# Attention scores of the first block in split-precision passes, differential maps combined before the transposes, and q/k made head by head

## The reference, cut to what matters

```python
s = jnp.einsum("bhcqd,bhcsd->bhcqs", qb, k_b).astype(jnp.float32) * scale_b
p = jax.nn.softmax(s, axis=-1)
a = p[:, :, 0] - lam * p[:, :, 1]
return jnp.einsum("bhqs,bhsv->bhqv", a.astype(v_b.dtype), v_b)
```

## Time and profile before

| what | value |
|---|---|
| median of three runs | 3435.35 us |
| span of the profiled execution | 3426.4 us |
| difference of the two, taken as what lies around the span | 8.95 us |
| TensorE busy | 3252.0 us, 95% of the span |
| VectorE busy | 1119.9 us, 33% |
| ScalarE busy | 995.3 us, 29% |
| GpSimd busy | 279.3 us, 8% |
| share of TensorE in the chain that ended last | 89% |

### The profile page before, as it was taken

One profiled execution on the slowest core, in us unless ns is written; L12 is line 12 of the kernel. 1 busy time (PEld: TensorE's weight loads), 2 busy tenths in 40 slices (PEclk: granted clock), 3 DMA queues, 4 the chain that ended last, 5 costly groups with the idle time before them and its releaser, 6 DMA issues.

```text
span 3426.4 us, 35084 instructions
## 1 busy us (share of the span) xinstructions
PE 3252.0 (95%) x14020; PEld 2219.0 (65%) x14020; DVE 1119.9 (33%) x1827; ACT 995.3 (29%) x1607; POOL 279.3 (8%) x268
## 2 busy tenths in 40 slices
PE   7999998999989999989999999979998999989997
PEld 6866564888878656658887555544666433468886
DVE  2624332333226343233332233344333100043322
ACT  4355441222233545322221223333222100022222
POOL 4480000000032700000000000000000000000000
PEclk8999999999989999999999999989998999989999
DMA  4221121333222211123323201102111121123331
GB/s 105 79 80 38 38 75 37 99 98 88 85 82 76 74 38 53 47 78 96 93 84 92 80 14 36 37 1 62 37 37 50 25 74 49 49 62 98 95 90 62
DMA packets 340274, 221.98 MB, mean 65 GB/s; under 512 B 8364, under 2 KB 334892, under 8 KB 340112
## 3 DMA queue, kind: packets, MB, share of 16 engines
q1 hardware_dynamic: 337360, 214.65, 21.6%
q0 software_dynamic: 2224, 2.99, 0.8%
q10 hardware_dynamic: 528, 2.10, 0.2%
HBM read 217.62 MB, written 2.10 MB: 64 GB/s over the span
## 4 chain that ended last, share of the span: by engine, by line
PE 89%; DVE 5%; ACT 4%; issue 1%; DMA 1%; DVEq 0%; ACTq 0%; SPq 0%
PE ps L591 83%; PE ps L602 4%; PE ps L618 2%; DVE R L1691 1%; ACT R L1204 1%; DVE xL L1687 0%; DVE x_lows L1687 0%; DMA ident<-in_c_ident 0%; PE ps L945 0%; DMA R<-in_ctx 0%; ACT R L1200 0%; ACT L1193 0%; DVE R L1780 0%; DVE R L1762 0%; DVE wL L1713 0%
## 5 line engine op out<-in xcount | busy, mean ns | idle before, releaser
L591 PE MATMUL ps<-R 128*128 128x64 f32 (+6 forms) x2272 | 519.6, 372 | 29.5 <-ACT R L1204 8.7
L591 PEld LDWEIGHTS ps<-R 128*128 128x128 f32 (+3 forms) x2272 | 306.1, 192 | 243.8 <-issue 137.1
L591 PE MATMUL ps<-xH,wH 128*128 128x512 f32 x1056 | 417.5, 395 | 21.9 <-DVE xL L1687 21.9
L591 PE MATMUL ps<-U,ring 128*128 128x512 f32 (+5 forms) x960 | 406.8, 575 | 12.3 <-ACT R L1410 12.3
L1204 ACT ACTIVATE R<-ps 128x512 f32<-128x512 f32 (+9 forms) x504 | 248.7, 493 | 578.7 <-PE ps L591 514.6
L591 PE MATMUL ps<-xL,wH 128*128 128x512 f32 x1056 | 414.2, 392 | 0.0
L591 PE MATMUL ps<-xH,wL 128*128 128x512 f32 x1056 | 414.0, 392 | 0.0
L591 PE MATMUL ps<-R,ring 128*128 128x512 f32 x704 | 367.2, 676 | 2.9 <-DVE R L1927 1.6
L1354 ACT ACTIVATE wH<-raws 128x2048 fp32r<-128x2048 f32 (+1 forms) x114 | 192.9, 1692 | 569.0 <-PE ps L591 568.4
L591 PEld LDWEIGHTS ps<-U,ring 128*128 128x128 f32 (+2 forms) x960 | 179.6, 191 | 214.7 <-issue 189.5
L1713 DVE TENSOR_TENSOR wL<-raws,wH 128x2048 fp32r<-128x2048 f32 (+1 forms) x114 | 229.3, 2011 | 233.2 <-ACT wH L1354 226.3
(11 more groups left out here) (279 smaller groups left out, 3281.8 us busy)
## 6 DMA issues: line engine op xcount, KB each, us to landing
raws<-in_w_gate_up SPq DMA_DIRECT2D x88, 512.0 KB, 5.1
ring<-in_w_in SPq DMA_DIRECT2D x36, 1024.0 KB, 6.2
ring<-in_w_ada SPq DMA_DIRECT2D x24, 1024.0 KB, 5.1
raws<-in_w_down SPq DMA_DIRECT2D x32, 704.0 KB, 4.6
raws<-in_w_ffn_in SPq DMA_DIRECT2D x44, 512.0 KB, 5.2
ring<-in_w_in SPq DMA_DIRECT2D x34, 512.0 KB, 5.7
raws<-in_w_ffn_out SPq DMA_DIRECT2D x16, 704.0 KB, 4.7
ring<-in_w_o SPq DMA_DIRECT2D x5, 1280.0 KB, 5.9
```

The costliest lines, as they stand in the source:

```text
L591: return nc.tensor.matmul(o, a, b, start=first, stop=last)
```

## The change: what it does

1. **Scores.** q and k are kept in `QK_parts` as a high and a low part of type float32r. For diff and gqa (width 64) q's high part stands on rows 0 to 63 and its low part on rows 64 to 127 (for the other map of a diff head, the other way round); k's high part is copied to both halves of one slot and its low part to both halves of the next. A score tile is then two passes over 128 rows. For mla (width 96) it is three passes over 96 rows. The one float32 matmul of before goes.
2. **Diff maps.** The stage has 16 steps of two units. VectorE multiplies the second map's exponentials by a ratio and adds the first's (`combined`); then there is one set of transposes, one of copies and one of value products for both maps. `PX` has 4 buffers where `P3` had 3.
3. **q and k streamed.** The three bursts go. A head's q or k (an "item") is transposed into a bank of the D ring; ScalarE copies the high parts out (2 copies for a diff q, 4 for a diff k, 1 for a gqa q, 2 for a gqa k, 1 for mla) and VectorE then subtracts as many low parts. `items_beside` says at which step: diff heads 1 to 3 at steps 0, 1, 4, 5, 8 and 9 of the diff stage; gqa between the tiles of the `mla_w_uq` products; mla at steps 22 and 23 of gqa, at the start of mla and at 8 of its steps.
4. **Order.** gqa's pieces of `W_IN` come before the latents; the diff stage comes before the `mla_w_uq` and `mla_w_ukv` products; four modulation pieces are loaded before these two. A score waits only for its own bank (`score_bank`). The squares and the norm of the diff output are spread over steps of gqa and mla.

The diff, cut to its core:

```diff
+        def high_copies(item):
+            kind, h = item
+            if kind == "diff_q":
+                o = B_SLOTS[h % 2]
+                return [(r, r, o + c) for c, r in enumerate(HALVES)]
+            if kind == "diff_k":
+                o = B_SLOTS[h % 2] + 2
+                return [(r, to, o + 2 * c) for c, r in enumerate(HALVES) for to in HALVES]
+            if kind == "gqa_q":
+                return [(HALVES[0], HALVES[0], G_SLOTS[0] + h)]
+            if kind == "gqa_k":
+                return [(HALVES[0], to, G_SLOTS[1] + 2 * (h - GH)) for to in HALVES]
+            return [((0, AQK), (0, AQK), A_SLOTS[h % 2][0 if kind == "mla_q" else 2])]
+        def low_parts(item):
+            kind, h = item
+            out_ = []
+            for n, (r, to, slot_) in enumerate(high_copies(item)):
+                if kind in ("diff_q", "gqa_q"):
+                    out_.append((r, r, slot_, HALVES[1] if r == HALVES[0] else HALVES[0], slot_))
+                elif kind in ("diff_k", "gqa_k"):
+                    out_.append((r, r, slot_, to, slot_ + 1))
+                else:
+                    out_.append((r, r, slot_, r, slot_ + 1))
+            return out_
+        def items_beside(stage, j):
+            if stage == "diff":
+                h, t = j // TT + 1, j % TT
+                return b_items(h)[t:t + 1] if h < BH and t < 2 else []
+            if stage == "gqa":
+                return a_items(0)[j - 22:j - 21] if j >= 22 else []
+            h, t = (j + 7) // TT, (j + 7) % TT
+            return a_items(h)[t:t + 1] if 2 <= h < AH and t < 2 else []
...
-        W_IN = (quarter_pieces("diff_qk", c1, 2 * BH * BV) + quarter_pieces("latent", 0, c1)
-                + quarter_pieces("diff_v", c1 + 2 * BH * BV, BH * BV)
+        W_IN = (quarter_pieces("diff_qk", c1, 2 * BH * BV)
                 + quarter_pieces("gqa_q", c1 + 3 * BH * BV, GH * GD)
-                + quarter_pieces("gqa_kv", c1 + 3 * BH * BV + GH * GD, 2 * GK * GD))
+                + quarter_pieces("gqa_kv", c1 + 3 * BH * BV + GH * GD, 2 * GK * GD)
+                + quarter_pieces("latent", 0, c1)
+                + quarter_pieces("diff_v", c1 + 2 * BH * BV, BH * BV))
...
+            for a in range(4):
+                yield ada_piece(l * NADA + a)
...
+            def part_transposes(item):
+                kind, h = item
+                bank = db.fill(pe)
...
+                    ins = nc.tensor.transpose(bank[0:v_.shape[1], t * P:(t + 1) * P], v_, ident[:, :])
+                ins.then_inc(d_full, 1)
+                qk_banks.append(db.n)
+            def stacked_scores(o, q, t, k):
+                mm(o, QKP[:, q, t * P:(t + 1) * P], QKP[:, k, :], True, False)
+                return mm(o, QKP[:, q, t * P:(t + 1) * P], QKP[:, k + 1, :], False, True)
+            def split_scores(o, slots, t):
+                qh, ql, kh, kl = slots
+                mm(o, QKP[0:AQK, qh, t * P:(t + 1) * P], QKP[0:AQK, kh, :], True, False)
+                mm(o, QKP[0:AQK, ql, t * P:(t + 1) * P], QKP[0:AQK, kh, :], False, False)
+                return mm(o, QKP[0:AQK, qh, t * P:(t + 1) * P], QKP[0:AQK, kl, :], False, True)
...
+            def score_bank(u):
+                if u >= 3:
+                    pe.wait_ge(s_exp, u - 2)
+                return S_BANKS[u % 3][:, :]
...
+            def attend_diff():
+                nonlocal unit
+                u0, made = unit, len(qk_banks)
+                rows_taken = modulation()
+                def scores(i):
+                    h, c, t = i // 8, i % 2, i // 2 % 4
+                    pe.wait_ge(qk_ready, made + 2 * h + 2)
+                    o = B_SLOTS[h % 2]
+                    stacked_scores(score_bank(u0 + i), o + c, t, o + 2 + 2 * c).then_inc(s_full, 1)
+                for item in b_items(0):
+                    part_transposes(item)
+                for i in range(3):
+                    scores(i)
...
+                for j in range(N):
+                    if 2 * j + 3 < 2 * N:
+                        scores(2 * j + 3)
+                    pp.more(combined)
+                    transposes([PX[(u0 + 2 * j) % 4][:, s * P:(s + 1) * P] for s in range(TT)], P)
+                    transposed.append(ab.n)
+                    if 2 * j + 4 < 2 * N:
+                        scores(2 * j + 4)
+                    if j >= 1:
+                        values(j - 1, None, (VB + (j - 1) // TT * BV, VB + ((j - 1) // TT + 1) * BV), transposed)
+                    for item in items_beside("diff", j):
+                        part_transposes(item)
+                    if rows_taken:
+                        modulation_columns(rows_taken)
+                        rows_taken = None
+                    if j in ADA_AT["diff"]:
+                        rows_taken = modulation()
+                values(N - 1, None, (VB + (BH - 1) * BV, VB + BH * BV), transposed)
...
+                    scores(score_bank(u0 + j), j).then_inc(s_full, 1)
...
-                    transposes([T[:, t, h * P:(h + 1) * P] for t in range(TT)], P)
+                attend_diff()
+                pp.more(gT_ready, TT)
...
+                    for t in range(TT):
+                        part_transposes(next(keys))
+                        tokens_tile(ab, t, lambda k: cT[:, k, :], 3, slot(i, 3, 576), half * 288, 288)
...
+            def high(item):
+                nonlocal qk
+                act.wait_ge(d_full, qk_banks[qk])
+                bank = D_BANKS[(qk_banks[qk] - 1) % 2]
+                copies = high_copies(item)
+                for n, ((a, b), (c, d), slot_) in enumerate(copies):
+                    ap.do(f(QKP[c:d, slot_, :], bank[a:b, :], ACT.Copy), qk_high if n == len(copies) - 1 else None)
+                qk += 1
+            def expo(u):
+                act.wait_ge(s_max, u + 1)
+                ap.do(f(PX[u % 4], S_BANKS[u % 3][:, :], ACT.Exp, bias=nmax[:, u % 4:u % 4 + 1],
+                        accum_out=rsum[:, u % 8:u % 8 + 1]), s_exp)
...
+                for item in first if stage == "diff" else ():
+                    high(item)
+                for i in range(3 if maps == 2 else 2):
+                    expo(u0 + i)
+                for item in first if stage != "diff" else ():
+                    high(item)
                 for j in range(N):
-                    if j + 2 < N:
-                        expo(u0 + j + 2)
+                    if maps * j + maps + 1 < maps * N:
+                        expo(u0 + maps * j + maps + (1 if maps == 2 else 1))
                     bank = ab.take(act)
-                    copy_out(PTb[:, (u0 + j) % 2, :], bank[:, :], a_free)
+                    copy_out(PTb[:, j % 2, :], bank[:, :], a_free)
+                    if maps == 2 and 2 * j + 4 < 2 * N:
+                        expo(u0 + 2 * j + 4)
+                    for item in items_beside(stage, j):
+                        high(item)
                     if columns_due:
-                        bank = ab.take(act)
-                        copy_out(mod[:, 2 * ada:2 * ada + 2, :], bank[:, 0:4].rearrange("p (a b) -> p a b", b=2), a_free)
-                        ada += 1
+                        take_columns()
...
+            def low(item):
+                bank = db.take(dve)
+                vp.more(qk_high)
+                parts_ = low_parts(item)
+                for n, ((a, b), (c, d), hi, (e, g), lo) in enumerate(parts_):
+                    vp.do(v.tensor_tensor(QKP[e:g, lo, :], bank[a:b, :], QKP[c:d, hi, :].bitcast(F32), ALU.subtract),
+                          d_free if n == len(parts_) - 1 else None)
+                vp.also(qk_ready)
...
+                for item in b_items(0):
+                    low(item)
+                for i in range(3):
+                    rowmax(u0 + i)
+                for j in range(N):
+                    u = u0 + 2 * j
+                    if 2 * j + 3 < 2 * N:
+                        rowmax(u + 3)
+                    dve.wait_ge(s_exp, u + 2)
+                    a_ = u % 4
+                    s_ = u % 8
+                    vp.do(v.reciprocal(rinv[:, a_:a_ + 2], rsum[:, s_:s_ + 2]))
+                    vp.do(v.tensor_scalar(ratio[:, 0:1], rsum[:, s_:s_ + 1], rinv[:, a_ + 1:a_ + 2], lams[:, l, 0:1], ALU.mult, ALU.mult))
+                    vp.do(v.scalar_tensor_tensor(PX[a_], PX[a_ + 1], ratio[:, 0:1], PX[a_], ALU.mult, ALU.add), combined)
+                    if 2 * j + 4 < 2 * N:
+                        rowmax(u + 4)
+                    if j >= 1:
+                        post(j - 1)
+                    for item in items_beside("diff", j):
+                        low(item)
+                post(N - 1)
...
+                def output_squares(j):
+                    if j % 5 == 2 and j // 5 < TT:
+                        o = O[:, j // 5, 384:896]
+                        vp.do(v.tensor_tensor(vtmp[:, 0, 0:512], o, o, ALU.mult))
```

(43 more changed lines are left out.)

270 lines of the change are left out of this document (138 added, 132 removed).

## The result

The changed kernel takes 3470.09 us (median of 4 runs, 3467.49 to 3472.77) against 3435.38 (3433.83 to 3438.79) for the kernel before: a ratio of 1.0101, 95% interval 1.0087 to 1.0115, 34.7 us slower. The profiled execution had a span of 3470.4 and took 3472.77 as a whole.

What follows compares the result with a forecast made beforehand. TensorE's own work was taken to bound the old attention stages, and a serial chain the new diff stage. Diff losses 37 + 45.6 less 2 x 24.4 gained elsewhere give +34 on 3435: 3469 us, range 3400 to 3498.

Steps and rivals of the forecast that it cites:

- the one forecast: Whole kernel: slower, 3442 to 3480 us, diff stage a chain mostly at half clock; chance 0.50.
- The diff stage as a chain: Diff stage: transposes, scores, row maxima and combine run in series; 152 us a layer, 2 more in layer 0.
- The pieces: Diff stage: 18 us to first combine; steps at full and half clock: plain 4.6, 6.8; q 7.6, 9.4; k 10.3, 12.1.
- A modulation adds 3.9 at full clock, 5.7 at half: Diff stage: three modulations add 3.9 us each at full clock, 11.7 together; at half clock they take 17.
- Clock: Diff stage: TensorE at half clock except five plain steps after a modulation; 126 us at full clock, 162 at half.
- Rival (a): Diff stage stays at full clock, 126 us (+2 in layer 0); kernel 3403 us; break-even at 135.6 a layer; chance 0.22.
- Outside diff, -24.4 a layer: Gqa, mla, mla_w and removed bursts: 24.4 us gained per layer, against 167.8 + 22.2 before.
- The new order, 0: Reordering W_IN and SyncE's queue, with modulation pieces loaded ahead of mla_w_uq, was costed at nothing.
- Layer 0's two extra microseconds: Layer 0's diff stage: 2 us added because GpSimd's rotation of gqa q/k slows VectorE's early combines.
- The upper end of 0.991 us: Combine on VectorE: priced at 0.752 us, with 0.991, the low part while GpSimd works, as upper end.
- The sum.: Whole kernel: diff losses 37 + 45.6 less 2 x 24.4 gained elsewhere give +34 us.
- The base.: Kernel before: profiled span 3426.4 us, 8.95 below the median of runs; +34 was added to the median 3435.

Runs made afterwards that it cites:

- e1: Changed kernel with only the combination of diff maps undone, the 32 maps run one by one again: 3376.45 us, 0.9835 of the kernel before.
- e2: Changed kernel with VectorE's combine of step j moved ahead of the row maximum of map 2j+3: 3412.04 us, ratio 0.9935 to the kernel before.
- e6: Changed kernel with 4, 8, 16 and 4 useless TensorE passes by step of a diff head, ahead of the wait for the combine: 3441.02 us, ratio 1.0023.
- e7: Changed kernel without q and k items for diff heads 1 to 3, whose scores read head 0's slots: 3410.07 us, ratio 0.9934.
- e3: As e2, with the subtractions of a q/k item also moved behind the combine of the next step: 3378.83 us, ratio 0.9841.

## Why the prediction was right, and where it was not

3469 was forecast and 3470.09 measured. The case that came is the one forecast. But part of the closeness is luck, so step by step, against the profiles of before. The sum has a slip to begin with: 162 - 11 is 151 and not 152, so its own terms give 3467.

- **The diff stage as a chain** (154 and 152 us): 152.4 and 150.7. e1 and e2 show it directly: breaking the series in either of two ways returns 94 and 58 us. The pieces: start 18 to the first combine, measured 18.2 to the transposes in layer 1 and 20.2 in layer 0; q 7.6 to 9.4, measured 8.6 to 9.1; k 10.3 to 12.1, measured 12.3; plain 4.6 to 6.8, measured 4.62 with the clock at 1.00 (e6) and 6.68 with it at 0.50 (e7), and 6.2 for the two of the changed kernel, which had half clock for 3.4 us.
- **A modulation adds 3.9 at full clock, 5.7 at half.** Neither price was measured by itself. With it a step is forecast at 8.5 us at full clock and 12.5 at half; measured are 11.25 in the changed kernel and 10.9 in e6, both between the two, with half clock for 6.1 and 5.4 us. The plain step behind it has the modulation's columns on top, 5.04 for 4.6.
- **Clock** (half but for five steps; 36 us between 126 and 162): this term was mis-sized. Half clock held for 81.7 of 150.7 us in layer 1 and for 88.7 of 152.4 in layer 0, well short of all but five plain steps. Its price was about right: e6 gives 0.25 and 0.22 us for a microsecond at half clock, where 36 / 162 = 0.22. So the clock cost some 20 us in layer 1 and not 26. What made up for it is the stage at full clock throughout: from e6 an estimate is 139.6 - 37.5 x 0.25 = 130, and 126 was forecast. That the two errors cancel is luck. Rival (a)'s premise, a clock of 1.00, did not occur; the estimate of 130 is under its point of decision, 135.6. The Trainium skill (TensorE: Matmul & The Clock Gate, on PSUM-queue cycling) tells of a bf16 kernel with small idle times between its groups of matmuls, whose clock swings between the levels. The trace agrees, with 0.70 and 0.73 in the two stages, 0.64 in a k step and 1.00 in the plain step behind a modulation.
- **Outside diff, -24.4 a layer**: -25.1 and -25.8 (306.1 - 116.0 = 190.1 and 296.2 - 106.4 = 189.8 before, 165.0 and 164.0 after). gqa unit 1.75, measured 1.74; mla 1.98, measured 1.99; `mla_w` 28.4, measured 25.8 and 25.9, because it ran at full clock from its start, which I had not assumed; the first gqa transposes waited 3.75 us, 2.45 more than before where 1.5 was forecast; 1.8 us of short waits at the seam from gqa to mla were not in the sum.
- **The new order, 0**: wrong by 2 us in layer 0. The diff stage's first modulation waits 2.06 us for cvec's Silu, which ScalarE runs behind the last copies of the projection and a table load of 1.28 us, from 194.42 to 194.64. Before, the Silu was as late (194.32 to 194.53), but the burst and the `mla_w` products stood ahead of the first modulation, which came at 220.6. So it is the move of the diff stage ahead of `mla_w` that costs this, not the order of the pieces of `W_IN`.
- **Layer 0's two extra microseconds** for GpSimd: 152.4 against 150.7 fits by chance, since 2.06 of the 152.4 are the wait of the point above. GpSimd's rotation of the gqa q/k ended 26 us into the stage, and one combine fell beside it: 1.47 us, all others take 0.75, so it cost 0.7. Timeline of VectorE and of GpSimd in the changed kernel:

```profile
211.27 1.47 DVE L1776 SCALAR_TENSOR_TENSOR R<-R 128x512 f32<-128x512 f32 x1
220.60 0.75 DVE L1776 SCALAR_TENSOR_TENSOR R<-R 128x512 f32<-128x512 f32 x1
```

```profile
211.19 0.99 POOL L494 TENSOR_TENSOR R<-R,C 128x384 f32<-128x384 f32 x1
```

The upper end of 0.991 us that the prediction took from the earlier trace rows is no price of one instruction. It is the mean of twelve of 0.69 us and two of 2.27 and 3.31; the first of these two began while GpSimd ran a subtraction (36.64 to 41.15). Timeline of VectorE in the kernel before:

```profile
39.43 2.27 DVE L1687 TENSOR_TENSOR x_lows<-R,U_parts 128x512 fp32r<-128x512 f32 x1
...
42.52 0.69 DVE L1687 TENSOR_TENSOR x_lows<-R,U_parts 128x512 fp32r<-128x512 f32 x1
```

- **The sum.** The attention parts came to +11.4 and +18.5 = +29.9, where +34 was forecast: diff lost 36.4 and 44.3 for 37 and 45.6, and the rest of the layers gained 25.1 and 25.8 for 24.4. What filled the gap was not in my account at all: the untouched rest took 2023.9 us, against 2011.5 and 2015.0 in the two profiles of before. By spans the changed kernel is 39.0 us behind the second profile of before: 0.5 ahead of the first attention, 11.0 and 18.4 in the two, 0.3 between them, 8.9 behind.
- **The base.** I took 8.95 us to lie around the profiled span. In the runs since, 1.7 to 2.4 lie around it (3433.26 with 3431.4, 3472.77 with 3470.4). So the profiled execution of before was probably a short one, by about 7 us, and not one with more around it; its own time is not on record.

So the mechanism was shown (e1, e2, e3, e7), and the plain, q and k steps at full clock came within 0.2 us of the forecast (4.62, 7.76 and 10.46 in e6, the last with 1.5 us at half clock). That the total came within 1 us was luck, since the share of the clock, the stage at full clock, the wait in layer 0, the slip in the sum and the rest of the kernel erred with both signs.

## What to carry to other kernels

Folding two results into one saves work only on the engine that is relieved; it puts a wait for both in front of the next step. Before doing it, write down for each engine what stands ahead of that wait in program order: here one row maximum on VectorE, ahead of the combine for no need of its own, held scores, modulation and combine in one series and cost 58 us. In a stage in which three engines take turns, price small helpers (copies, subtractions, items) at full length, and compare with the version that is not folded but has had the same care: here it was as fast, 3353 against 3350 us.

## What the runs showed of the hardware

- The clock costs time far from the place that is changed: the same 6908 matmuls took 2011.5 to 2024.1 us in the rest of the kernel, and in the two profiles of before and in the changed kernel's the difference was half of the difference in time spent at 0.50, to within 1 us (167, 174 and 191 us of it).
- Half clock came without long waits: in e7 TensorE never waited longer than 2.15 us behind the first transposes, and the granted clock was 0.50 for 69.9 of those 107.4 us.
- Work on TensorE that gives nothing can pay: 32 passes per head ahead of a wait took 29 us off the kernel.
- Ahead of the stage's first exponential ScalarE loads a table for 1.28 us, and TensorE, which needs the bank that this exponential empties, is then idle for 1.32 us; the kernel before has the load too, at the start of its stage.

```profile
1144.95 1.28 ACT L1358 ACT_TABLE_LOAD   x1 [5.11 <-DVE nmax L1740]
```
